# Attention probabilities scaled by their inverse sums on VectorE before the transposes, in place of a matmul that spreads the inverse sums over the output

## The reference, cut to what matters

```python
def block(qi):                                    # kind A; B adds a bias, C a mask and a sink
    s = jnp.einsum('bqhgd,bkhd->bhgqk', qi, k_all)
    p = softmax_f32(s, v_all.dtype)
    return jnp.einsum('bhgqk,bkhd->bqhgd', p, v_all)
...
ux = jnp.concatenate([ya, yb, yc_], axis=-1) * jax.nn.silu(px[9])
x = x + gate[:, None, :] * (ux @ w_out)
```

## Time and profile before

| | |
|---|---|
| median of 3 executions | 3602.55 us (3596.44 to 3605.22) |
| span of the profiled execution | 3611.0 us |
| TensorE busy | 3363.7 us, 93% |
| VectorE busy | 935.5 us, 26% |
| ScalarE busy | 784.5 us, 22% |
| the two attention layers | about 108 to 1730 us of the span |

### The profile page before, as it was taken

How to read it: one execution, slowest core, us unless ns; L and a number is a source line. 1 busy time by engine, 2 the same in 40 slices (tenths; PEclk the granted TensorE clock), 3 DMA queues, 4 the chain that set the end, 5 groups by cost and what they waited for, 6 DMA issues and landing times.

```text
span 3611.0 us, 37201 instructions
## 1 busy us (share of the span) xinstructions
PE 3363.7 (93%) x15156; PEld 1792.0 (50%) x15156; DVE 935.5 (26%) x1884; ACT 784.5 (22%) x1302; POOL 11.4 (0%) x24
## 2 busy tenths in 40 slices
PE   6999999999999989999989999799999998799998
PEld 3566655666555555565444444444444343444443
DVE  1222222234112222234146432211111252211112
ACT  2222334233122223423134200200000213100001
POOL 0000000000000000000000000000000000000000
PEclk8999899999999989999999999899999998899999
DMA  6122111121112222211210200389999522499997
GB/s 251 71 74 110 69 47 47 59 94 47 59 58 111 84 75 94 94 59 59 92 42 23 82 0 33 141 322 410 410 410 410 223 70 112 198 410 410 410 410 282
DMA packets 130310, 583.36 MB, mean 162 GB/s; under 512 B 9136, under 2 KB 9136, under 8 KB 110096
## 3 DMA queue, kind: packets, MB, share of 16 engines
q1 hardware_dynamic: 128496, 572.81, 40.5%
q0 software_dynamic: 1696, 8.85, 0.8%
HBM read 579.52 MB, written 2.10 MB: 161 GB/s over the span
## 4 chain that ended last, share of the span: by engine, by line
PE 84%; ACT 7%; DMA 4%; DVE 3%; issue 2%; SPq 0%; DVEq 0%; ACTq 0%
PE BIG L567 62%; PE OP L791 4%; PE PT L776 4%; PE BIG L1099 3%; DMA W<-in_exp_w 3%; PE BIG L766 3%; PE BIG L762 2%; PE BIG L765 2%; PE OP L796 2%; ACT ARENA L1229 1%; ACT ARENA L1237 1%; PE MODP L607 1%; PE PT L567 1%; DMA XC<-in_x 1%; ACT ARENA L1409 0%
## 5 line engine op out<-in xcount | busy, mean ns | idle before, releaser
L567 PE MATMUL BIG<-HT,W 128*128 128x512 f32 (+1 forms) x2720 | 1029.6, 538 | 25.0 <-ACT HT L1157 16.9
L567 PEld LDWEIGHTS BIG<-HT,W 128*128 128x128 f32 x2720 | 516.7, 192 | 509.1 <-issue 477.3
L567 PE MATMUL BIG<-ARENA 128*64 128x512 f32 (+1 forms) x2688 | 476.1, 459 | 2.5 <-DVE ARENA L1820 2.5
L567 PE MATMUL BIG<-W,ARENA 128*64 128x512 f32 (+1 forms) x1680 | 405.6, 595 | 27.4 <-ACT ARENA L1409 18.5
L567 PEld LDWEIGHTS BIG<-ARENA 128*64 128x64 f32 (+1 forms) x2688 | 246.3, 162 | 224.7 <-issue 224.7
L567 PE MATMUL BIG<-ARENA,W 128*128 128x512 f32 (+1 forms) x832 | 318.6, 545 | 4.9 <-ACT ARENA L1370 4.9
L567 PEld LDWEIGHTS BIG<-W,ARENA 128*64 128x64 f32 (+1 forms) x1680 | 145.1, 141 | 272.0 <-issue 249.8
L1237 ACT ACTIVATE ARENA<-PT 128x512 f32<-128x512 f32 (+3 forms) x240 | 153.6, 640 | 471.0 <-PE PT L776 471.0
L567 PEld LDWEIGHTS BIG<-ARENA,W 128*128 128x128 f32 x832 | 158.4, 191 | 164.0 <-issue 157.8
L1563 DVE TENSOR_REDUCE STAT<-BIG 128x1 f32<-128x768 f32 (+6 forms) x240 | 178.5, 744 | 209.1 <-PE BIG L766 203.4
L1847 DVE SCALAR_TENSOR_TENSOR XC<-BIG,MOD,XC 128x512 f32<-128x512 f32 x128 | 90.2, 746 | 417.6 <-PE BIG L1099 417.6
(11 more groups left out here) (218 smaller groups left out, 2075.0 us busy)
## 6 DMA issues: line engine op xcount, KB each, us to landing
W<-in_exp_w SPq DMA_DIRECT2D x192, 1024.0 KB, 15.4
ARENA<-in_exp_w SPq DMA_DIRECT2D x192, 1024.0 KB, 17.5
W<-in_units SPq DMA_DIRECT2D x156, 1024.0 KB, 6.8
ARENA<-in_bias_b POOLq DMA_DIRECT2D x16, 448.0 KB, 3.5
XC<-in_x SPq DMA_DIRECT2D x1, 3072.0 KB, 21.4
out_t<-HT SPq DMA_DIRECT2D x8, 256.0 KB, 2.2
XC<-in_ctx POOLq DMA_DIRECT2D x1, 1024.0 KB, 8.0
CONST<-in_consts SPq DMA_DIRECT2D x1, 897.0 KB, 4.7
```

The lines of the kernel that those rows point to most:

```text
L567: ins = pe.matmul(out, lhsT, rhs, start=start, stop=stop)
```

## The change

`schedule` gets a further item N(n), which stands first in iteration n. In it VectorE waits for E(n), inverts the one sum of the step, and multiplies the step's 256 to 768 probabilities per row in `PROB` by it, in place. T(n) on TensorE now waits for that multiplication and no longer for E(n) directly. RB, its copy, the matmul L796 and the second multiplication of the output (L1581) go; O's last matmul of V signals VectorE itself.

```diff
     for n in range(-1, last + 2):
+        if 0 <= n <= last:
+            order.append(("N", n))
         if n + 1 <= last:
             order.append(("S", n + 1))
...
                     elif what == "T":
                         i, h, t = steps[x]
-                        pe.wait_ge(big_free[score_use[x] % 2], me.over(score_use[x]))
+                        pe.wait_ge(probs_scaled, me.next("probs_scaled"))
...
-
-                        pe.wait_ge(sums_inverted, me.next("sums_inverted"))
-                        pe.matmul(OP[:, P:2 * P], RB.rearrange("p h d -> p (h d)"), const("ident"),
-                                  start=True, stop=True).then_inc(o_filled, 1)
...
+                        last.then_inc(o_filled, 1)
...
-                        if x % 2:
-
-                            dve.wait_ge(big_free[score_use[x] % 2], me.over(score_use[x]))
-                            dve.wait_ge(big_free[score_use[x - 1] % 2], me.over(score_use[x - 1]))
-                            c = x % 4 - 1
-                            link(dve.reciprocal(STAT[:, 8 + c:10 + c], STAT[:, 4 + c:6 + c]))
-                            dve.tensor_copy(RB, STAT[:, 8 + c:10 + c].unsqueeze(2).to_broadcast([P, 2, HD]))\
-                                .then_inc(sums_inverted, 1)
+                    elif what == "N":
+                        i, h, t = steps[x]
+                        a, b = score_span(PAIRS[i][0], t)
+                        dve.wait_ge(big_free[score_use[x] % 2], me.over(score_use[x]))
+                        link(dve.reciprocal(STAT[:, 8 + x % 4:9 + x % 4], STAT[:, 4 + x % 4:5 + x % 4]))
+                        probs = PROB[:, x % 2, 0:min(b, NA) - a]
+                        dve.tensor_scalar(probs, probs, STAT[:, 8 + x % 4:9 + x % 4], None, ALU.mult)\
+                            .then_inc(probs_scaled, 1)
                     elif what == "O":
...
-                        link(dve.scalar_tensor_tensor(y, like_query_tile(i, t, OP[:, 0:P]), 0.5,
-                                                      query_tile(i, t, SG[:, i % 2, :]), ALU.mult, ALU.mult))
-                        dve.tensor_tensor(y, y, like_query_tile(i, t, OP[:, P:2 * P]), ALU.mult)\
+                        dve.scalar_tensor_tensor(y, like_query_tile(i, t, OP[:, 0:P]), 0.5,
+                                                 query_tile(i, t, SG[:, i % 2, :]), ALU.mult, ALU.mult)\
                             .then_inc(y_ready, 1)
```

10 lines of the change are left out of this document (5 added, 5 removed).

## The result

The changed kernel takes 3733.84 us (median of 4 runs, 3731.61 to 3739.64) against 3599.49 for the kernel before (4 runs, 3593.35 to 3605.22): ratio 1.0391, 95% interval 1.0358 to 1.0424 (the ratio is not the quotient of the two medians, which is 1.0373 and lies in the interval). It is slower, as forecast, but by 134 us where I had forecast some 70, and it lies above the range. The profiled execution took 3733.42 us, with a span of 3731.2 us.

A forecast was written before the change was run, and what follows sets the result against it. TensorE, busy 93% of the span, was taken as the bound. Delays of 96 us less 43 gained make +53, plus 15 for the clock: span 3679, median 3670 us, 1.9% slower; range of 8 in 10, 3630 to 3720.

The forecast's parts named there:

- the delays: In front of T in the attention layers: new waits for the scaling, forecast to sum to 96 us.
- the clock: TensorE in the attention layers: added waits lower its granted clock, costing up to 40 us, taken as 15.
- Removed: L796 behind O on TensorE: its removal gains 46 us, 43 effective; VectorE's removed work is worth nothing by itself.
- Added: N between E and T: reciprocal 0.15 us, scaling 0.35 to 0.62 us by width, each handover about 0.05 us.
- the rival with one element per cycle: VectorE's scaling in N runs slower, making N 0.27 to 0.4 us longer: about 3710 us, chance 8%.
- item 1: Odd steps with nothing inserted in front of T: 34 delays of 0.9 us each, 30 us.
- item 2: Odd steps behind a rotation: 15 delays of T, 1.35 us each, 20 us.
- item 3: Odd steps behind the gate projection: 11 delays of T, 1.0 to 1.8 us, 14 us.
- item 4: T behind the norms of q and k: 8 delays, mostly 1.4 to 1.75 us, 12.5 us.
- item 5: Even steps: the maximum stands behind the last step's N, so E starts later; 0.1 to 0.8 us per step, 17 us.
- the faster rival: VectorE has real room, N ends before TensorE needs it, and the 46 us remain: about 3557 us, chance 5%.
- the clock becomes the larger term: Waits at nearly every second step lower TensorE's clock more often, 40 us or more: 3695 to 3720 us, chance 20%.

The follow-up runs named there:

- e3_matmul_back: The changed kernel with a matmul of constants of L796's shape behind each O, its result unused: 3775.8 us, ratio 1.051 to the kernel before.
- e2_no_norm: The kernel before without L796, the copy to RB and the multiplication L1581, so the output is not normalized: 3569.91 us, ratio 0.9944.
- e6_twice: The changed kernel with a second scaling of the probabilities, by 1.0, in front of the first: 3835.62 us, ratio 1.0639 to the kernel before.
- e5_eighth: The changed kernel, scaling only the first eighth of each row of probabilities: 3685.94 us, ratio 1.0232 to the kernel before.
- e4_fill4: The changed kernel with four unused matmuls of constants in front of T at each of 76 places where T waits: 3659.76 us, ratio 1.018.
- e10: The changed kernel with O divided by key tiles, first half at the even step, second at the next odd one: 3730.8 us, ratio 1.0395.
- e1: The changed kernel, with VectorE writing the scaled probabilities into a buffer nobody reads and T waiting only for E: 3634.19 us, ratio 1.0105.
- e15: The changed kernel with two unused matmuls of constants in front of T at each of 76 places where T waits: 3699.66 us, ratio 1.0278.
- e9: The changed kernel with three unused matmuls in front of T at each of 100 even steps, where T seldom waits: 3774.15 us, ratio 1.0504.
- e13: The changed kernel with four unused matmuls, each on 64 rows and 64 columns, at each of 76 places where T waits: 3697.74 us, ratio 1.0301.
- e7_split_after: The changed kernel with O cut in two by heads, each head done in its own step's turn: 3693.15 us, ratio 1.0245.

## Why the prediction was wrong in size

Its direction and the place of the waits held. Two terms had the wrong size, in opposite directions: the delays were some 26 us too high, the clock 74 to 85 too low, so a part of the second error was hidden by the first.

**Removed.** L796 was put at 46 us, 43 of them effective. The work fell by 39.4 us, and e3_matmul_back puts it at 34 to 42. That VectorE's relief is worth nothing also held: in e2_no_norm it is busy 67 us less than before (453.5 in the stretch of the earlier trace rows, 386.7 there), and the gain is no more than L796 explains.

**Added.** N's durations came out within 0.01 us, by the slope of L1590 and an offset between its own and that of L1637. The middle was a guess, and e6_twice shows why it fits: at 512 elements the scaling without a per-row operand takes 428 ns, with one 488, and L1590 with two 545. The Trainium skill, VectorE: DVE Perf Modes, section "The perf-mode tier table", two elements per cycle for this operation, agrees with the 134 ns per 256 elements; the rival with one element per cycle (8%) is out, since 621 ns at 768 are far from L1522's 1018. The handover is 0.06 us at 1844.32 (0.05 forecast).

**The delays, item by item.** From the idle time before each T of both traces, by what stands ahead of it, in us before and after: nothing ahead at odd steps 12.5 and 35.2 (item 1, forecast +30, found +22.7); behind a rotation 0 and 18.1 in 14 waits (item 2, forecast 20); behind the gate 0 and 13.0 in 14 waits (item 3, forecast 14); behind norms 0 and 24.0 in 8 waits, of which the rotation's matmul gives back 8.3 (19.5 in 9 waits before, 11.2 in 2 now), leaving 15.7 (item 4, forecast 12.5); even steps 2.5 and 9.2 (item 5, forecast 17, found +6.7). The prediction also said of the faster rival that with 0.45 us of N or less the delays would fall below 46; that was too easy, for e5_eighth, whose N is 0.57 us by the same count, still has 74.1 us in front of the transposes. The forecast sum of delays is 96, and the T's idle time rose by 85.6. Less the 8.3 and some 8 that other waits lost, the stretch has 69.5 more. So this term was 26 us too high. In part that is the clock again: where it is low, TensorE arrives later, and N is done before it comes, as at 1817.80. Delay and clock loss are two forms of the same microseconds, and the sum treated them as separate.

**The clock: the step that failed.** The prediction says: "If the added waits raised the share by 5 points, 80 us more would run at the lower level ... that loses up to 40 us ... I take 15." The share went from 191 of 1621 us (12%) to 381 of 1740 (22%), 10 points, and cost 88.8 us by the profiles. The executions profiled differ by 3731.2 - 3611.0 = 120 us, the medians by 134; the other 14 us are in the choice of the execution of before, a long one (3611.0) at a low clock for this kernel (0.951; the 44 others have a median of 0.957). With 69.5 - 39.4 = +30 of idle time and work, the clock's part in the medians is about 100 us, seven times my figure. The clocks of all executions say the same: from 0.957 to 0.9265 is some 240 us more at 1.2 GHz, of which about 100 to 115 are lost. The rival "the clock becomes the larger term" described this, with 20% and an upper end of 3720 that was its own size carried over from the same guess.

Two things were wrong in it. I took the number of points from one comparison inside the kernel before, at 0.86 against 0.94, then discounted it since short waits at the same places "left the clock alone in most of layer 1". But those waits were 0.3 us, the new ones average 1.2. And I bounded the cost by the share that I had supposed. The observed pattern of 28% of low clock from 400 to 600 us was itself in the trace: applied to the whole stretch it would have been 16 points, 260 us at the low clock and up to 130 us of loss. The range had to reach there. The Trainium skill, TensorE: Matmul & The Clock Gate, section "What's actually happening", on which the prediction weighed the term, has the gate follow how busy the engine has been; the 74 us that e4_fill4 wins back with useless matmuls agree with it. The 42 us of e10 without idle time at 1.2 GHz show that a busy engine by the profile's count is not enough.

**What would have shown it.** Of the tests that the prediction named, the idle time rose by 69, under the 80 to 110 it gave; 81 waits, not 110; VectorE's 1008 against "about 1010"; and the granted clock moved by 0.05 where over 0.03 was to mean that I was wrong.

**What is shown and what stays open.** Shown by runs: T's wait for the scaling costs 100 us, N's place on VectorE without it 64 (e1, e2); the clock loss grows and shrinks with the length of N (e5, e6) and is given back by work in the waits (e4, e15), much less by work elsewhere (e9), and not by the missing matmul (e3); matmuls on a part of the array give back less (e13). Open: by what rule the clock is granted; why e1_scratch loses some 50 us of clock for 16 us of idle time over e2_no_norm; why e10's last pair stays low, for which partial use of the array is a guess that e13 supports, and that the last pair of before and e7_split_after speak against as the only cause; and the scaling by another engine or from another buffer was not tried.

## What to carry to other kernels

An engine that is busy 26% of the time has no room at a place where a second engine waits for it: count what is added to the shortest chain between two steps, and not the share. Where TensorE works without gaps, price a new wait twice, for its length and for the clock: here 69 us of idle time came with 89 us of clock loss, and the upper bound should come from the worst stretch of the kernel's own trace, carried over all of it. If TensorE's busy time rises with fewer matmuls, look at the granted clock before any other cause, and test it with filling matmuls in the wait, which showed it in one run.

## What the runs showed of the hardware that I had not expected

Matmuls of two heads that each fill 64 columns of the array run beside each other when they alternate: their 2112 records take 161.2 us alternating and 302.3 us one head after the other, at 302 and 289 ns each.

TensorE stayed at 1.2 GHz for 42 us in which it was never idle, on matmuls that use half of the array for the most part, right behind 42 us at 2.4 GHz with 3.85 us of idle time (e10). The kernel before ran the same kinds of matmul for 27 us at 2.4 GHz with 3.4 us of idle time (888 to 915 us). And filling matmuls on a quarter of the array, as long as the wide ones, gave back 70 instead of 107 us of clock loss (e13, e4).

Useless work made a kernel faster: some 300 filling matmuls of 128x128 in front of the waiting transposes took 74 us off 3733.84. A per-row operand of VectorE's scaling costs about 0.06 us at 512 elements: 428 ns without, 488 with one (e6), 545 with two (L1590).
